# Norm statistics: joining and splitting the squares on POOL, two single-pass matmuls at the fourth piece, the root read from PSUM

## The reference

```python
def rmsnorm(x, g):
    xf = x.astype(jnp.float32)
    r = lax.rsqrt(jnp.mean(xf * xf, axis=-1, keepdims=True) + EPS)
    return (xf * r).astype(x.dtype) * g
...
    for l in range(DEPTH):
        h = h + 0.5 * swiglu(rmsnorm(h, ffn1_norm[l]), ffn1_w_gu[l], ffn1_w_down[l])
        h = h + mixer(rmsnorm(h, mix_norm[l]), w_in[l], ret_gn[l], w_ret_proj[l],
                      w_sb_proj[l], w_out[l], pos, valid)
        h = h + 0.5 * swiglu(rmsnorm(h, ffn2_norm[l]), ffn2_w_gu[l], ffn2_w_down[l])
    h = rmsnorm(h, final_norm)
```

## Time and profile before

| | |
|---|---|
| median of 3 runs | 1330.44 us (1330.10 to 1330.62) |
| the profiled execution | 1329.98 us, its span 1328.2 us |
| mean granted clock of PE | 0.998 of full speed |
| PE busy | 1302.9 us, 98% of the span, 10440 matmuls |
| DVE busy | 855.7 us, 64% |
| ACT busy | 641.9 us, 48% |
| POOL busy | 39.2 us, 3%, of which 20 adds of squares 33.7 us |

### The profile page before, as it was taken

How to read it: one execution, slowest core, us unless ns; L and a number is a source line. 1 busy time by engine, 2 the same in 40 slices (tenths; PEclk the granted TensorE clock), 3 DMA queues, 4 the chain that set the end, 5 groups by cost and what they waited for, 6 DMA issues and landing times.

```text
span 1328.2 us, 26426 instructions
## 1 busy us (share of the span) xinstructions
PE 1302.9 (98%) x10440; PEld 1293.9 (97%) x10440; DVE 855.7 (64%) x996; ACT 641.9 (48%) x820; POOL 39.2 (3%) x31
## 2 busy tenths in 40 slices
PE   6999999999999999999999999999999999999996
PEld 6999999999999999999999999999999999999996
DVE  6666556766765776665566665577567667766654
ACT  5444445545555554444444444455455565544441
POOL 2000001000000010000010000010000000000000
PEclk9999999999999999999999999999999999999999
DMA  7655655554334556555545555545543345665561
GB/s 278 192 174 174 175 176 150 182 167 134 113 112 128 159 173 187 174 177 175 175 159 189 174 174 174 175 148 186 175 124 118 124 147 171 192 189 188 174 199 55
DMA packets 61205, 219.53 MB, mean 165 GB/s; under 512 B 6992, under 2 KB 8272, under 8 KB 61008
## 3 DMA queue, kind: packets, MB, share of 16 engines
q1 hardware_dynamic: 60704, 217.93, 52.3%
q10 hardware_dynamic: 432, 0.59, 0.2%
HBM read 217.44 MB, written 1.05 MB: 164 GB/s over the span
## 4 chain that ended last, share of the span: by engine, by line
PE 92%; DVE 4%; issue 2%; ACT 1%; DMA 0%; POOL 0%; DVEq 0%; SPq 0%; ACTq 0%; POOLq 0%
PE bank L736 29%; PE bank L737 28%; PE bank L738 28%; DVE w_lo L453 1%; PE bank L949 1%; PE bank L903 1%; PE bank L923 1%; PE bank L936 1%; PE bank L832 1%; ACT act L360 1%; PE bank L815 1%; DMA raw<-stream 0%; DVE gv L622 0%; DVE r L475 0%; DVE act L549 0%
## 5 line engine op out<-in xcount | busy, mean ns | idle before, releaser
L453 DVE TENSOR_TENSOR w_lo<-raw,w_hi 128x1024 fp32r<-128x1024 f32 x408 | 507.8, 1250 | 299.1 <-ACT w_hi L288 294.9
L736 PE MATMUL bank<-xh,w_hi 128*128 128x272 f32 (+1 forms) x2240 | 646.2, 288 | 12.3 <-DVE xl L467 11.2
L288 ACT ACTIVATE w_hi<-raw 128x1024 fp32r<-128x1024 f32 x408 | 427.7, 1056 | 445.2 <-PE bank L738 441.8
L737 PE MATMUL bank<-xl,w_hi 128*128 128x272 f32 (+1 forms) x2240 | 642.1, 287 | 0.0
L738 PE MATMUL bank<-xh,w_lo 128*128 128x272 f32 (+1 forms) x2240 | 640.5, 286 | 0.0
L736 PEld LDWEIGHTS bank<-xh,w_hi 128*128 128x128 f32 x2240 | 423.3, 189 | 14.2 <-DVE xl L467 9.8
L737 PEld LDWEIGHTS bank<-xl,w_hi 128*128 128x128 f32 x2240 | 421.8, 188 | 0.2
L738 PEld LDWEIGHTS bank<-xh,w_lo 128*128 128x128 f32 x2240 | 421.6, 188 | 0.0
L736 PE MATMUL bank<-gh,w_hi 128*128 128x272 f32 (+1 forms) x1024 | 293.1, 286 | 0.0
L737 PE MATMUL bank<-gl,w_hi 128*128 128x272 f32 (+1 forms) x1024 | 292.1, 285 | 0.0
L738 PE MATMUL bank<-gh,w_lo 128*128 128x272 f32 (+1 forms) x1024 | 291.9, 285 | 0.0
(11 more groups left out here) (108 smaller groups left out, 635.7 us busy)
## 6 DMA issues: line engine op xcount, KB each, us to landing
raw<-stream SPq DMA_DIRECT2D x408, 512.0 KB, 3.6
table<-tables SPq DMA_DIRECT2D x1, 2000.0 KB, 9.6
out<-h SPq DMA_DIRECT2D x4, 256.0 KB, 2.7
h<-tokens ACTq DMA_DIRECT2D x2, 272.0 KB, 5.2
h<-tokens SPq DMA_DIRECT2D x2, 272.0 KB, 5.6
dec<-squares SPq DMA_DIRECT2D x1, 192.0 KB, 7.8
square<-squares SPq DMA_DIRECT2D x1, 128.0 KB, 7.7
gain<-gains ACTq DMA_DIRECT2D x1, 28.0 KB, 4.3
```

Source lines behind the costliest of these rows:

```text
L288: eng.activation(w_hi[:, slot, :], raw[:, slot, :], ACT.Copy).then_inc(hi_ready, 1)
L453: eng.tensor_tensor(w_lo[:, slot, :], raw[:, slot, :], w_hi[:, slot, :].bitcast(F32), ALU.subtract).then_inc(lo_ready, 1)
L736: pe.matmul(out, wh, hi, start=first, stop=False)
L737: pe.matmul(out, wh, lo, start=False, stop=False)
```

## The change

In the six norms that open a sub-layer, POOL gets three more operations after its adds (`split_squares`): ssq's halves joined into ms, the same joined and rounded to fp32r as ms_hi, and the remainder ms_lo. PE sums ms_hi and ms_lo with two single-pass fp32r matmuls, now ahead of block 0 of the fourth piece, and waits there for `ssq_split`. ACT takes the root of the bank itself, with scale 1/8 and bias eps, and DVE's ms is gone. The final norm keeps its four fp32 matmuls at their place and has the new root.

```diff
--- before.py
+++ after.py
@@ -120,6 +120,8 @@
         sqh = sb("sqh", [P, 2, T])
         ssq = sb("ssq", [P, 2, T])
         ms = sb("ms", [P, T])
+        ms_hi = sb("ms_hi", [P, T], F32R)
+        ms_lo = sb("ms_lo", [P, T], F32R)
         r = sb("r", [P, T])
         dec = sb("dec", [P, SCORES])
         ro = sb("ro", [P, T])
@@ -188,7 +190,7 @@
 
         h_new, x_scaled, xh_ready, x_ready = sem("h_new"), sem("x_scaled"), sem("xh_ready"), sem("x_ready")
         sq_ready, ssq_added, ssum_done = sem("sq_ready"), sem("ssq_added"), sem("ssum_done")
-        ms_ready, rms_ready, r_ready = sem("ms_ready"), sem("rms_ready"), sem("r_ready")
+        ssq_joined, ssq_split, rms_ready, r_ready = sem("ssq_joined"), sem("ssq_split"), sem("rms_ready"), sem("r_ready")
 
         gate_scaled, gate_act, up_gated = sem("gate_scaled"), sem("gate_act"), sem("up_gated")
         g_val, gh_ready, g_ready = sem("g_val"), sem("gh_ready"), sem("g_ready")
@@ -263,9 +265,19 @@
                     pool.wait_ge(ssq_added, rnd * ADDS + (p - 1))
                 pool.tensor_tensor(ssq[:, :, :], ssq[:, :, :], sqh[:, :, :], ALU.add).then_inc(ssq_added, 1)
 
+            def split_squares(rnd):
+
+                pool.wait_ge(ssq_added, rnd * ADDS + ADDS)
+                for whole_or_hi in (ms, ms_hi):
+                    pool.tensor_tensor(whole_or_hi[:, :], ssq[:, 0, :], ssq[:, 1, :], ALU.add).then_inc(ssq_joined, 1)
+                pool.wait_ge(ssq_joined, 2 * rnd + 2)
+                pool.tensor_tensor(ms_lo[:, :], ms[:, :], ms_hi[:, :].bitcast(F32), ALU.subtract).then_inc(ssq_split, 1)
+
+            pool.wait_ge(pads_ready, 1)
             with pool.Fori(0, 3 * DEPTH) as rnd:
                 for p in range(1, PAIRS):
                     add_squares(rnd, p)
+                split_squares(rnd)
             for p in range(1, PAIRS - 1):
                 add_squares(3 * DEPTH, p)
 
@@ -310,8 +322,8 @@
                 squares_of_h(rnd, p, q0)
 
             def rms(rnd, q0):
-                eng.wait_ge(ms_ready, rnd + 1)
-                eng.activation(r[:, q0:T], ms[:, q0:T], ACT.Sqrt).then_inc(rms_ready, 1)
+                eng.wait_ge(ssum_done, rnd + 1)
+                eng.activation(r[:, q0:T], bank[:, 4, q0:T], ACT.Sqrt, scale=1.0 / DC, bias=eps[:, 0:1]).then_inc(rms_ready, 1)
 
             def ffn(l, f):
                 fi = l * 2 + f
@@ -469,8 +481,6 @@
 
             def norm_factor(rnd, q0):
 
-                eng.wait_ge(ssum_done, rnd + 1)
-                eng.tensor_scalar(ms[:, q0:T], bank[:, 4, q0:T], 1.0 / DC, EPS, ALU.mult, ALU.add).then_inc(ms_ready, 1)
                 eng.wait_ge(rms_ready, rnd + 1)
                 eng.reciprocal(r[:, q0:T], r[:, q0:T]).then_inc(r_ready, 1)
 
@@ -745,12 +755,15 @@
 
             def sum_of_squares(rnd, q0, final=False):
 
-                pe.wait_ge(squares_in, 32)
-                pe.wait_ge(ssq_added, rnd * ADDS + (ADDS - 1 if final else ADDS))
-                pe.matmul(bank[:, 4, q0:T], ones, ssq[:, 0, q0:T], start=True, stop=False)
-                mm = pe.matmul(bank[:, 4, q0:T], ones, ssq[:, 1, q0:T], start=False, stop=not final)
-                if final:
-
+                if not final:
+                    pe.wait_ge(masks_ready, 1)
+                    pe.wait_ge(ssq_split, rnd + 1)
+                    pe.matmul(bank[:, 4, q0:T], ones_r, ms_hi[:, q0:T], start=True, stop=False)
+                    mm = pe.matmul(bank[:, 4, q0:T], ones_r, ms_lo[:, q0:T], start=False, stop=True)
+                else:
+                    pe.wait_ge(ssq_added, rnd * ADDS + (ADDS - 1))
+                    pe.matmul(bank[:, 4, q0:T], ones, ssq[:, 0, q0:T], start=True, stop=False)
+                    pe.matmul(bank[:, 4, q0:T], ones, ssq[:, 1, q0:T], start=False, stop=False)
                     pe.wait_ge(sq_ready, rnd * PAIRS + PAIRS)
                     pe.matmul(bank[:, 4, q0:T], ones, sqh[:, 0, q0:T], start=False, stop=False)
                     mm = pe.matmul(bank[:, 4, q0:T], ones, sqh[:, 1, q0:T], start=False, stop=True)
@@ -780,8 +793,8 @@
 
 
                 first_unit(l * 3 + 2 * f, lambda half, before: gate(base + half, half, before), q0, f)
-                up(base + 2, 0, {2 if f else 0: lambda: sum_of_squares(l * 3 + 2 * f, q0)})
-                up(base + 3, 1)
+                up(base + 2, 0)
+                up(base + 3, 1, {0: lambda: sum_of_squares(l * 3 + 2 * f, q0)})
                 with pe.Fori(1, ITERS) as it:
                     pe.wait_ge(gate_scaled, fi * ITERS + it)
                     gate(base + it * 4, 0)
@@ -843,7 +856,7 @@
                 for s in range(2, MIX):
                     u = s // 2
                     before = {}
-                    if s == 2:
+                    if s == 3:
                         before[0] = lambda: sum_of_squares(rnd, 0)
                     hd = (s - SB0 - 2) // 2
                     if (s - SB0) % 2 == 0 and 0 <= hd < HEADS:
```

## The result

| | before | after |
|---|---|---|
| median | 1330.58 us (5 runs) | 1345.9 us (5 runs, 1344.45 to 1347.14) |
| the profiled execution, its span | 1329.98, 1328.2 us | 1347.14, 1345.4 us |
| ratio, 95% interval | | 1.0113 (1.0101 to 1.0126) |
| mean granted clock of PE | 0.998 | 0.992 |

The change costs 15.3 us, against a forecast of 11.3; 1345.9 lies above the range's 1344.2. The direction is right and the size is not.

The account below looks back on a forecast made before the run. PE held 92% of the last-ending chain, but the chain from sum through root to piece 4 or the mixer's reciprocal was taken to bind. Round terms summed to +11.3 us, forecasting 1341.7 us, range 1335.5 to 1344.2.

Parts of the forecast that it names:

- So a wait of 2.0 us appears in each FFN round: FFN openings: piece 4 starts at t + 5.28, the fourth piece ends at t + 3.25, so PE waits 2.0 us.
- PE's restart: Rounds 0 and 3: after a wait PE's first matmul lasts 0.39 us instead of 0.28 or 0.29, priced at 0.10.
- my rivals or bounds: POOL keeps port 1338.8 (0.22); POOL in time 1335.8 (0.10); slower POOL beyond 1344.2 (0.08); faster 1325.3 (0.05); no change 1330.4 (0.05).
- The sum's move: Sum one piece later: 0.455 us to its reader, then 4.83 us from root start to piece 4 in FFNs.
- The mixer's chain: Rounds 1 and 4: a later reciprocal delays everything until PE resumes; +2.5 us each, PE's own savings buy nothing.
- POOL's split: Three POOL operations at 0.70 us each, semaphores of 0.15 within POOL and to PE: 2.4 us from free port to t.
- The turns: DVE and POOL alternate on the port: a third w_lo costs 1.13 us in rounds 1 and 4, round 0's casts 0.63.
- The tail: Final norm: DVE's ms removed, ACT reads the bank itself; -0.45 us.
- PE's saving: Two fp32 matmuls become two single-pass ones: 0.665 us less in six rounds, 4.0 us, were PE alone the bound.

Follow-up runs that it names:

- waits filled with 14: The changed kernel with 14 unread matmuls more at the end of the fourth piece of each FFN opening: 1341.45 us, ratio 1.0083.
- weights ahead: The changed kernel with the weight split of piece 4 (w_hi, w_lo) ahead of the root and the reciprocal in each FFN: 1338.22 us.
- the fp32 sums: The changed kernel without POOL's split: two fp32 matmuls on ssq at the fourth piece, root from PSUM: 1343.33 us.
- the joined version: Root from PSUM and weights ahead, plus POOL joining ssq's halves in FFN rounds and PE summing once in fp32: 1325.24 us, ratio 0.9961.
- root from PSUM and weights ahead: The kernel before with the root from PSUM and, in each FFN, piece 4's weight split ahead of root and reciprocal: 1327.41 us.
- the version filled with six: The changed kernel with 6 unread matmuls more at the end of the fourth piece of each FFN opening: 1341.58 us.

## Why the prediction was wrong

The terms can be read one by one: the distance from POOL's first add of one round to that of the next, less the same distance before (round 0: 185.03 - 10.29 before, 187.16 - 10.55 filled, 188.59 - 10.42 after; the last row is from round 6's first add to the end of the span).

| round | forecast | waits filled with 14 | changed kernel |
|---|---|---|---|
| 0 | +2.35 | +1.87 | +3.43 |
| 1 (mixer) | +2.5 | +2.41 | +2.42 |
| 2 | +1.1 | +1.20 | +2.72 |
| 3 | +1.7 | +1.76 | +3.27 |
| 4 (mixer) | +2.5 | +2.37 | +2.38 |
| 5 | +1.6 | +1.67 | +3.22 |
| final | -0.45 | -0.34 | -0.37 |
| sum | +11.3 | +10.9 | +17.1 |

With the clock held the sum stands within 0.4 us, and that kernel's 1341.45 is near the forecast's 1341.7. Part of that closeness is luck: round 0 came 0.5 lower than forecast, and small excesses elsewhere make up for a part of it. The four FFN rounds differ by 1.56, 1.52, 1.51 and 1.55 us, 6.1 in the profiled execution with its four slow stretches; in the median 4.45.

- **The step that failed** is the price of the wait in "So a wait of 2.0 us appears in each FFN round": I priced the wait at its length and 0.10 for PE's restart. The wait is there (1.9 to 2.1 idle, 2.2 to 2.35 from matmul to matmul), but PE's clock can fall behind it, and then 1.5 us more go in each. None of my rivals or bounds had a term for it, so the range ended below the result. That the idle time is the cause is shown by filling it (14 or 6 matmuls) and by shortening it (weights ahead); why the clock stayed up behind two of the four waits with the fp32 sums is not known.
- *Could the trace of before have told?* Not the price: the longest idle times inside it, 1.70 us near the start and 1.0 us at 249.08, were followed by the full clock. But a kernel whose PE, once started, is never idle for 2 us gives no licence to leave the clock out when 2 us of idle time are being added; that bound was missing.
- *The sum's move* was right: 2.2 to 2.35 us from matmul to matmul in the four FFN rounds, and 4.88 from root to piece 4 for 4.83.
- *The mixer's chain* was right: reciprocal and everything to the next PE wait moved by 2.4 in each, forecast 2.5.
- *POOL's split*: 0.77 per operation for 0.70. A semaphore between two POOL operations was 0.07 where I took 0.15, so the whole was right to 0.1. The turns are as in the forecast, except round 0: there the two casts waited for POOL (0.86 and 0.93 us instead of 0.28 and 0.35) but hardly held it up (ms_hi took 0.83, not 1.3), and the round came to +1.87 for 2.35.
- *The tail*: -0.34 to -0.37 for -0.45; the root from PSUM takes 0.47 us there, not 0.42, which is about half of the difference.
- *PE's saving* of 4.0 us could show only in rounds where PE waits for nothing, and there was none; the joined version shows what is to be had of such a saving when the sum's reader has slack.

## What to carry to other kernels

Where one engine is busy nearly all the time, a reduction's place in its stream is set by the chain behind the result, not by what the reduction costs there: count from the sum to the first instruction that needs it, and see what stands in front of it on each engine. Price a wait that you add on PE as its length plus a possible slow stretch behind it (here 1.5 us behind waits of 1.9 to 2.1), and check the granted clock by stretches, not over the span (0.992 against 0.998 hid 4 to 6 us). If the wait can't be removed, matmuls that nobody needs can stand in it: six of them, 0.75 us, were enough here. Take a bundle of edits apart: here one of three was a gain of 3.1 us and the others lost 18.

## What was not expected of the hardware

- After an idle time of PE of 1.9 to 2.1 us (2.2 to 2.35 between matmuls) the granted clock fell to the lower level in eight of eight cases in the two profiled executions of the changed kernel and in two of four with the fp32 sums, at the same place and with the same work around it; it fell once after 1.84 us (root from PSUM and weights ahead). In the changed kernel it cost 1.5 us each time, by the table of rounds. After idle times of up to 1.55 us (mixers, and the version filled with six) and after the 1.70 us in the kernel before it did not fall in any profiled execution.
- The fall shows not at the wait but after work resumed, and each time at another distance: in round 0 the matmuls still start 0.125 apart for 1.5 us, from 29.22 to 30.70; in round 3 those from 699.92 on, 0.8 us after the first, are 0.23 apart; in round 5 the clock is down 0.4 us after it.
- The run's spread is a sign of it: 1344.4 to 1347.7 for the changed kernel, under 0.7 us for each version whose waits are filled.
- Whether DVE or POOL goes first can hang on the program around an operation. With POOL's loop written out instead of `Fori` (the joined version), the last add took 1.36 or 1.37 us in all six rounds, not 2.4 as in the earlier trace rows. Round 1 has no join and the same work in both versions: POOL's add started at 216.03, 0.05 ahead of DVE's w_lo, where with `Fori` it started 0.03 behind it and took 2.41. It was worth 0.05 us in each mixer; in the FFN rounds it was not measured apart from the join.
